# Sparse branch of a hybrid decoder layer: probabilities scaled by GpSimd before their transposes, outputs split straight from PSUM

## The reference

```python
_, idx = lax.top_k(score, topk)          # 128 keys for every query
s = jnp.einsum('bthd,btkd->bthk', qb, ks) * (HEAD_DIM ** -0.5)
s = s - slopes * dist
p = masked_softmax(s, dist >= 0)          # p = exp(s - max) / sum
return jnp.einsum('bthk,btkd->bthd', p, vs)
...
merged = sigmoid(gate_a_m) * (o_a @ w_up_a) + sigmoid(gate_b_m) * (o_b @ w_up_b)
x = x + merged @ w_out
h2 = rms_norm(x, g_mlp)
x = x + square(relu(h2 @ w_ff1)) @ w_ff2
```

## Time and profile before

| | |
|---|---|
| median of 3 runs | 742.16 us (742.0 to 742.4) |
| profiled execution | 741.73 us |
| its span, first to last instruction | 740.0 us |
| granted TensorE clock, mean | 1.000 |
| VectorE busy | 585.3 us (79%) |
| ScalarE busy | 437.7 us (59%) |
| GpSimd busy | 177.1 us (24%) |

### The profile page before, as it was taken

One profiled execution on the slowest core, in us unless ns is written; L12 is line 12 of the kernel. 1 busy time (PEld: TensorE's weight loads), 2 busy tenths in 40 slices (PEclk: granted clock), 3 DMA queues, 4 the chain that ended last, 5 costly groups with the idle time before them and its releaser, 6 DMA issues.

```text
span 740.0 us, 12690 instructions
## 1 busy us (share of the span) xinstructions
PE 731.7 (99%) x4686; PEld 651.4 (88%) x4686; DVE 585.3 (79%) x1079; ACT 437.7 (59%) x803; POOL 177.1 (24%) x192
## 2 busy tenths in 40 slices
PE   9999999999999999999999999999999999999998
PEld 9998977877997778777888899999999888799997
DVE  5478889769986877666767988988887788897987
ACT  7768377756767897555356555566556544533341
POOL 3110336523555545300012422222220000000000
PEclk9999999999999999999999999999999999999999
DMA  9621221111111111102533333333332332323332
GB/s 336 252 81 50 76 87 58 57 29 58 53 54 47 49 58 58 57 31 85 199 115 96 105 114 105 96 97 104 114 115 86 100 100 86 108 92 114 115 123 77
DMA packets 22861, 71.00 MB, mean 96 GB/s; under 512 B 2448, under 2 KB 5648, under 8 KB 22544
## 3 DMA queue, kind: packets, MB, share of 16 engines
q1 hardware_dynamic: 22800, 70.19, 30.5%
HBM read 68.08 MB, written 2.10 MB: 95 GB/s over the span
## 4 chain that ended last, share of the span: by engine, by line
PE 83%; DVE 8%; ACT 5%; issue 2%; DMA 1%; POOL 0%; DVEq 0%; SPq 0%; POOLq 0%
PE psum L2143 23%; PE psum L2145 22%; PE psum L2144 22%; PE psum L2151 5%; PE psum L2340 4%; PE psum L2317 2%; PE psum L2318 2%; DVE w_lo L1481 1%; DMA x2T<-in_xT 1%; ACT w_hi L1056 1%; DVE prob L1695 1%; ACT h L1056 1%; ACT q_st L1056 1%; DVE x2T L1848 1%; PE psum L2158 1%
## 5 line engine op out<-in xcount | busy, mean ns | idle before, releaser
L1056 ACT ACTIVATE w_hi<-stage 128x512 fp32r<-128x512 f32 (+4 forms) x149 | 114.7, 777 | 30.6 <-PE psum L2145 26.8
L2143 PE MATMUL psum<-hT_hi,w_hi 128*128 128x256 f32 (+1 forms) x324 | 113.5, 350 | 0.8 <-DVE q_st L1637 0.6
L2144 PE MATMUL psum<-hT_lo,w_hi 128*128 128x256 f32 (+1 forms) x324 | 107.3, 331 | 0.0
L2145 PE MATMUL psum<-hT_hi,w_lo 128*128 128x512 f32 (+1 forms) x264 | 90.6, 343 | 0.0
L1481 DVE TENSOR_TENSOR w_lo<-stage,w_hi 128x1024 fp32r<-128x1024 f32 (+4 forms) x58 | 56.8, 985 | 41.3 <-ACT w_hi L1056 37.1
L1056 ACT ACTIVATE w_hi<-s_sum 128x1024 fp32r<-128x1024 f32 x46 | 48.7, 1060 | 54.3 <-PE psum L2145 52.0
L2144 PE MATMUL psum<-a_lo,w_hi 128*128 128x512 f32 (+1 forms) x224 | 77.0, 344 | 0.0
L1243 ACT ACTIVATE prob<-prob,neg_max 128x128 f32<-128x128 f32 (+3 forms) x96 | 53.8, 560 | 35.4 <-DVE neg_max L1695 34.7
L1020 POOL TENSOR_TENSOR w_lo<-stage,w_hi 128x512 fp32r<-128x512 f32 x46 | 59.6, 1300 | 36.2 <-ACT w_hi L1056 36.0
L2143 PE MATMUL psum<-t_hi,w_hi 128*128 128x256 f32 x240 | 67.9, 283 | 0.0
L2144 PE MATMUL psum<-t_lo,w_hi 128*128 128x256 f32 x240 | 67.9, 283 | 0.0
(11 more groups left out here) (316 smaller groups left out, 2042.4 us busy)
## 6 DMA issues: line engine op xcount, KB each, us to landing
stage<-in_panels SPq DMA_DIRECT2D x104, 512.0 KB, 3.6
xT_in<-in_xT SPq DMA_DIRECT2D x8, 260.0 KB, 5.1
x_in<-in_x SPq DMA_DIRECT2D x4, 512.0 KB, 7.3
phi<-in_phi SPq DMA_DIRECT2D x2, 1024.0 KB, 6.8
x2T<-in_xT SPq DMA_DIRECT2D x1, 2048.0 KB, 9.0
stage<-in_panels SPq DMA_DIRECT2D x8, 212.0 KB, 5.1
stage<-in_panels SPq DMA_DIRECT2D x4, 408.0 KB, 3.1
stage<-in_panels SPq DMA_DIRECT2D x4, 384.0 KB, 5.0
```

The lines of the kernel that those rows point to most:

```text
L1056: return nc.scalar.activation(dst, src, ACT.Copy, scale=scale)
L2143: mm(dst, a_h, b_h, start=start, stop=False)
L2144: mm(dst, a_h, b_l, start=False, stop=False)
L2145: return mm(dst, a_l, b_h, start=False, stop=stop)
```

## The change

For DSA (WEIGHED = DSA, and only this branch) "inv", "fac" and "close" are gone. In their place each pair of units gets a step "weigh": in step u = 66, 68, ... 96, behind QK of unit u and ahead of the transposes of unit u-3, VectorE waits for the exponentials of units u-2 and u-1 and takes the reciprocals of their sums (128x2); GpSimd waits for that and multiplies both `prob` buffers, 128 x w each, in place, by the reciprocal of their row. TensorE's transposes of a DSA unit wait for its multiplication instead of its exponential. oT_hi and oT_low of branch A read the bank of O itself, and oT_low frees it; `o_a` is gone. OA_PLACES becomes 85, 88, 93. The waits of the first up tile of A and of the load of x change with the semaphore.

```diff
-OB_PLACES, OA_PLACES = (70, 80, 81, 82), (85, 95, 96)
+OB_PLACES, OA_PLACES = (70, 80, 81, 82), (85, 88, 93)
...
     for ti in range(NU // H):
-        at_unit(ti * H + 9, "inv", ti, at=early)
-        at_unit(ti * H + 10, "fac", ti)
+        if ti // TT < WEIGHED:
+            at_unit(ti * H + 9, "inv", ti, at=early)
+            at_unit(ti * H + 10, "fac", ti)
...
         if u < NU:
             step("qk", u)
+        if 2 <= u <= NU and u % 2 == 0 and units[u - 1][0] >= WEIGHED:
+            step("weigh", u - 2)
         if 0 <= u - T_LAG < NU:
             step("pT", u - T_LAG)
...
-        if u >= TAKEN_AT and (u - TAKEN_AT) % H == 0:
+        if u >= TAKEN_AT and (u - TAKEN_AT) % H == 0 and (u - TAKEN_AT) // H < DSA * TT:
             step("close", (u - TAKEN_AT) // H)
...
-    step("close", NU // H - 1)
...
-        def out_tile(m, tt):
-
-            return (o_b[:, tt, :, :], tt) if m else (o_a[:, tt % 2, :, :], TT + tt)
+        def out_tile(eng, m, tt):
+
+            if m:
+                return o_b[:, tt, :, :], tt
+            ps = wait_full(eng, ("O", DSA * TT + tt))
+            return ps.rearrange("p (k t) -> p k t", k=4), TT + tt
...
-            sp.wait_ge(oT_lo_done, 2 * TT)
+            for tt in (TT - 2, TT - 1):
+                wait_drained(sp, ("O", DSA * TT + tt))
...
+                elif kind == "weigh":
+                    u0, = a
+                    w = (units[u0][1] + 1) * P
+                    pool.wait_ge(pair_inv, (u0 - WEIGHED * TT * H) // 2 + 1)
+                    for u in (u0, u0 + 1):
+                        prob = probs[u % PROBS][:, 0:w]
+                        nc.gpsimd.tensor_tensor(prob, prob, row_inv[:, u:u + 1].to_broadcast([P, w]), ALU.mult)\
+                            .then_inc(weighed, 1)
...
+                elif kind == "weigh":
+                    u, = a
+                    br, tt, h = units[u]
+                    ve.wait_ge(exp_done, u + 2)
+                    inv = row_inv[:, u:u + 2]
...
+                    else:
+                        nc.vector.reciprocal(inv, row_sum[:, u:u + 2]).then_inc(pair_inv, 1)
...
                 elif kind == "oT_low":
                     m, tt = a
-                    src, n = out_tile(m, tt)
+                    src, n = out_tile(ve, m, tt)
                     ve.wait_ge(oT_hi_done, n + 1)
...
+                    if m:
+                        ins.then_inc(oT_lo_done, 1)
+                    else:
+                        drained(ins, ("O", DSA * TT + tt))
...
                 elif kind == "pT":
                     u, = a
-                    te.wait_ge(exp_done, u + 1)
+                    if units[u][0] >= WEIGHED:
+                        te.wait_ge(weighed, u - WEIGHED * TT * H + 1)
+                    else:
+                        te.wait_ge(exp_done, u + 1)
```

More of the change, by code:

```diff
@@ L162, in hybrid_layer @@
     SLC, WIN, DSA = range(3)
+    WEIGHED = DSA
     units = [(br, tt, h) for br in (SLC, WIN, DSA) for tt in range(TT) for h in range(H)]
@@ L551, in hybrid_layer @@
         relu = place("relu", [P, RELUS, S], Z + 59 * K)
-        o_a = place("o_a", [P, 2, 4, P], Z + 43 * K)
         cmp_e = place("cmp_e", [P, TT, H, CP], Z + 47 * K)
@@ L641, in hybrid_layer @@
         inv_done = sem("inv_done")
+        pair_inv = sem("pair_inv")
+        weighed = sem("weighed")
         fac_spread = sem("fac_spread")
@@ L1267, in _ @@
                     m, tt = a
-                    src, n = out_tile(m, tt)
+                    src, n = out_tile(se, m, tt)
                     if m:
@@ L1272, in _ @@
                         wait_drained(se, ("cmpO", tt))
+                        wait_drained(se, ("O", TT + tt))
                     else:
                         se.wait_ge(oT_lo_done, TT)
-                    wait_drained(se, ("O", TT * (1 if m else 2) + tt))
                     copy(oT_hi[m][:, :, tt * P:(tt + 1) * P], src).then_inc(oT_hi_done, 1)
@@ L1782, in _ @@
                     wait_drained(ve, ("cmpO", tt))
+                elif kind == "weigh":
[3 more added lines that the diff above has]
+                    inv = row_inv[:, u:u + 2]
+                    if br == WIN:
+                        link(nc.vector.reciprocal(inv, row_sum[:, u:u + 2]))
+                        tt_op(inv, inv, gates[:, tt, h:h + 2, 1 + WIN], ALU.mult).then_inc(pair_inv, 1)
+                    else:
+                        nc.vector.reciprocal(inv, row_sum[:, u:u + 2]).then_inc(pair_inv, 1)
                 elif kind == "inv":
@@ L1790, in _ @@
                     br, tt, _ = units[ti * H]
-                    wait_drained(ve, ("fac", ti))
+                    if br < WEIGHED:
+                        wait_drained(ve, ("fac", ti))
                     ps = wait_full(ve, ("O", ti)).rearrange("p (k t) -> p k t", k=4)
                     if br == WIN:
-                        link(tt_op(ps, ps, fac[:, :, :], ALU.mult))
+                        if br < WEIGHED:
+                            link(tt_op(ps, ps, fac[:, :, :], ALU.mult))
                         o = o_b[:, tt, :, :]
@@ L1797, in _ @@
                     else:
[L1798 to L1801, removed]
+                        ins = tt_op(o_b[:, tt, :, :], ps, fac[:, :, :], ALU.mult)
                     drained(ins, ("O", ti))
@@ L1805, in _ @@
                     m, tt = a
-                    src, n = out_tile(m, tt)
+                    src, n = out_tile(ve, m, tt)
                     ve.wait_ge(oT_hi_done, n + 1)
                     tok = slice(tt * P, (tt + 1) * P)
-                    tt_op(oT_lo[m][:, :, tok], src, oT_hi[m][:, :, tok].bitcast(F32), ALU.subtract)\
-                        .then_inc(oT_lo_done, 1)
+                    ins = tt_op(oT_lo[m][:, :, tok], src, oT_hi[m][:, :, tok].bitcast(F32), ALU.subtract)
+                    if m:
+                        ins.then_inc(oT_lo_done, 1)
+                    else:
+                        drained(ins, ("O", DSA * TT + tt))
                 elif kind == "split" and a[0] not in pool_panels:
@@ L2401, in _ @@
                     if what == "up" and i == 0 and k == 0:
-                        te.wait_ge(oT_lo_done, TT if m else 2 * TT)
+                        if m:
+                            te.wait_ge(oT_lo_done, TT)
+                        else:
+                            for tt in (TT - 2, TT - 1):
+                                wait_drained(te, ("O", DSA * TT + tt))
                     dst = open_bank(("tile", t)) if k == 0 else psum[:, bank[("tile", t)][0], :]
```

## The result

The changed kernel takes 750.7 us (median of 5 runs, 749.2 to 753.6); the kernel before, on the same chip, 742.2 (5 runs, 741.5 to 742.4). The ratio is 1.0121, 95% interval 1.0102 to 1.0139. The forecast was 749.7 us in a range of 744.5 to 753.0.

The account below looks back on a forecast made before the run. TensorE, busy throughout the sparse branch, was taken to bound the kernel: 741.73 - 2.7 (removed work and waits) + 6.5 (path waits) + 3.8 (queue) = 749.3 us, as a median 749.7. Own range 746.5 to 752, overall 744.5 to 753.0.

Parts of the forecast that it names:

- What bounds it: Sparse branch, 256 to 330 us: TensorE is busy for all 74.00 us, so every wait of it is paid in full.
- What goes: TensorE's time removed: four turnings of fac, 1.76 us, and two waits behind the branch, 0.9 us; 2.7 us gone.
- the four turnings: TensorE's transposes of fac at steps 74, 82, 90 and 98: 0.44 us each, 1.76 us in all, would go.
- the two places behind the branch: TensorE's waits ending at 333.27 and 339.43 shrink without the last close: 0.9 us gone, bounds 0 and 1.04.
- The path: QK of u+2, VectorE's add, reciprocal, multiplication, transposes of u: 2.7 us at 512, 1.9 at 256; six waits, 6.5 us.
- The queue: Units 66 to 78: multiplications stand behind GpSimd's older work, or VectorE is late: 3.8 us more, bounds 1.5 and 5.
- R1: Rival: GpSimd's older work finds other gaps, no queue term; 6.5 us of waits alone, 745.5 us, median 745.9; chance 0.18.
- The lock (R2): Rival: VectorE's two-SBUF-operand operations in the branch are held during GpSimd multiplications; 2 to 4 us more, 751.5 to 754; chance 0.15.
- more often than twice: Sign against the forecast, for R2: VectorE's oT_low or score taking over 1.5 us more than two times.
- R3: Rival: TensorE's waits don't occur, multiplication far faster or order different; only 2.7 us goes: 739.0, median 739.5; chance 0.07.
- R4: Rival: the waits just equal what goes, 742 us, with multiplications at copy price and GpSimd's queue free; chance 0.04.
- The sum: Profiled execution: 741.73 - 2.7 + 6.5 + 3.8 = 749.3 us; median 0.43 above that, 749.7 us.

Follow-up runs that it names:

- experiment 3: Changed kernel, but GpSimd scales the gates of branch A's tiles 3 to 7 behind the next pair of multiplications: 749.9 us, ratio 1.0117 to before.
- experiment 5: Changed kernel, but reciprocal and multiplication of unit u-2 given one by one ahead of QK of step u, not in pairs behind it: 746.7 us, ratio 1.0061 to before.
- experiment 7: Changed kernel with weighing unit by unit ahead of QK, as in experiment 5, but the multiplication on VectorE instead of GpSimd: 750.4 us, ratio 1.0112 to before.
- experiment 8: Changed kernel, but unit u-1 weighed singly in step u, behind the exponential, ahead of top-k: 744.1 us; with gate scalings behind as well, 743.4 us.

## Why the prediction was right, and where it was off

- **What bounds it.** Right: TensorE pays each wait, and none was made up for later.
- **What goes.** Priced at 2.7 us, it is 2.5 in the profile: the four turnings give 0.44, 0.46, 0.44 and 0.43 us (1.77, priced 1.76), the two places behind the branch 0.75 (priced 0.9), the first paired product 0.27 (not priced), and PV's wait for probT takes back 0.32. That last one is the step that failed. I treated a removed turning as pure gain and didn't ask what it covered: VectorE's copy of probT, which is then late by 0.2 to 0.3 us. Without the multiplication this stands at two PVs, and the gain is 2.3 us, which says the same. That the price came out close is in part luck: the gain at the paired product, where the transfer of x happened to land early, almost pays for the loss at PV.
- **The path.** Right to 0.1 us for each of the units 82 to 90, as its steps were read from rows: 0.61 + 0.24 + 1.10 at w = 512, where 0.61 + 0.26 + 1.08 had been set. (The recorded 1.9 at 256 stands for 1.96 at unit 78, whose QK is 384 wide, and 1.81 at 76.) The multiplication's price, a line through two rows of other shapes and forms, gave 1.04, 0.62 and 0.41 us, measured 1.042, 0.618 and 0.402; at 384 the mean is 0.884 for 0.83, with single ones at 0.83.
- **The queue.** Right in size (3.8 predicted; units 66 to 78 beyond their path 3.7: 1.55 + 0.71 + 0.12 + 0.35 + 0.93), but not in all its reasons. At unit 66 the gate's scaling is what the multiplication waits for; yet with it out of the way the whole loss reappears at unit 68 (experiment 3), because VectorE is the one that is late. At unit 76 GpSimd's queue has no part at all: GpSimd is idle, and waits for a reciprocal that VectorE could not give before the exponential of unit 77:

```profile
287.13 0.17 DVE L1808 RECIPROCAL row_inv<-row_sum 128x2 f32<-128x2 f32 x1 [0.23 <-ACT prob L1259]
...
287.38 1.19 POOL L1030 TENSOR_TENSOR prob<-prob,row_inv 128x256 f32<-128x256 f32 x2 [0.19 <-DVE row_inv L1808]
```

  Two units are inverted at once, so the first has to wait for the second's sum. In experiment 5, which inverts them one by one but also in another place, the jump at 76 is gone. The prediction had counted such a wait only for unit 68. Rival R1, no queue term, falls all the same.
- **The lock (R2).** Its sign appeared, not its price. Three of VectorE's four oT_low of branch B took over 1.5 us, the fourth 1.2, as this one in after:

```profile
292.33 1.30 POOL L1036 TENSOR_TENSOR w_lo<-stage,w_hi 128x512 fp32r<-128x512 f32 x1
...
292.45 1.72 DVE L1834 TENSOR_TENSOR oT_lo<-o_b,oT_hi 128x512 fp32r<-128x512 f32 x1
```

  Three of the four were held by a weight split and one by a multiplication, and no jump of TensorE's starts follows: VectorE had the slack there. The marker "more often than twice" was badly chosen; what counts is whether TensorE's next wait is for VectorE. Where VectorE was the last on the path, the lock did cost (experiments 5 and 7).
- **R3 and R4** fall: the path is 1.9 to 2.7 us, as the rows had it.
- **The sum.** 749.3 for a profiled execution; it took 749.16. In the profile, -2.5 and +10.3 give 7.8 (7.6 predicted), of which 0.5 is taken back by a start that was 0.54 us sooner in this execution, at 5 us and so outside of the change; that makes the 7.3 of the spans, and the total's fit to 0.1 us is luck. The median is 1.5 us above the best run: between the two profiles of after the late x transfer and the start make the difference, and the two longest runs have a lower mean clock. That was not foreseen: I had carried over from before that profiled execution and median lie 0.4 us apart.

## What to carry to other kernels

When a step is put between two engines that met before, write down its path from the last instruction that stands ahead of it in every in-order list, and compare that with what the bounding engine has to do in between; here that sum came out to 0.1 us in ten, though one of the nine waits had another cause than the one written down. Where the step stands in the lists decided more than how much it does: the same 32 multiplications cost 10.3 us of waits behind QK and 2.3 ahead of the top-k round with the gate scalings behind them, while cutting their width to two columns still left 6.2. Ask of each removed instruction what it covered, and of each large transfer whether its landing has slack, before a small difference of medians is put down to the change. And give a second edit to the kernel before as well, or its gain is booked to the first.

## What the runs showed of the hardware that was not expected

**The clock fell behind a single wait of about 2 us, in three executions.** Experiment 3's profile, by stretches (us, busy time of PE, PEld, DVE, ACT, POOL, granted clock, DMA share, GB/s), behind its wait at unit 68:

```profile
274.50:277.60 3.10, 3.10 (x9) 2.37 (x8) 1.44 (x1) 1.33 (x5) 0.90 (x1) 0.50 0.00 0
```

The clock is at the lower of its two levels, 1.2 GHz, while TensorE is busy throughout; eight 128x512 matmuls start 0.43 us apart instead of 0.23, which costs 1.6 us. The two-column profile shows the same behind its wait at 420, and experiment 7's behind that at unit 79. TensorE stood idle for 1.86, 1.85 and 2.10 us in these three. The length alone doesn't decide it: in after's profile it stood idle for 1.75 us at unit 78, in experiment 8's for 1.96 us in the MLP, and the granted clock stayed at 1.00. The longest runs of after (753.6) have a mean clock of 0.997 where the others have 1.0, which fits such a fall; their traces were not taken. The Trainium skill, page TensorE: Matmul & The Clock Gate, section "HAM oscillation — how this bites in real kernels", warns of idle gaps longer than any of these; in these three traces shorter ones came just ahead of the fall.

**One 2 MB transfer into SBUF took 8.3 to 10.6 us** for the same bytes, issued at the same point of the program. Four of the ten profiles of changed kernels with the transfer in its old place took over 10 us, the others 8.3 to 9.8. The kernel before took 9.0 in its one profile; a landing after 10.3 would add some 1.3 us, and its 67 runs lie between 741.2 and 742.8, so at most a few of them can have had one. What makes it long stayed open: the edits touch neither the transfer nor the panels around it, and only its effect was tested.
